# Keys and values of the second layer as two units of seven block products each, with five of the products inside the softmax steps

## The chip, the cores and the metric

The kernel runs on one core of a Trainium2 chip. The metric is the device time of one execution in microseconds (us). The engines are named as the profile names them: PE (TensorE, matrix products), DVE (VectorE), ACT (ScalarE), POOL (GpSimd) and SP (SyncE, which issues most DMA transfers). All arithmetic is in float32. One matmul of the program stands as two records in the trace.

## The reference

Two layers on 256 tokens of width 1024. Each layer is attention, then a layer norm, then a mixture of 32 experts, then a layer norm. The first layer's attention is of another kind; the change lies in the second layer's, which reads in the reference (cut):

```python
def nsa_attention(x, w_in, w_out, pos_k, pos_v, ck_w1, ck_w2, cv_w1, cv_w2, rel_bias):
    proj = x @ w_in
    sizes = [H * d] + [Hkv * d] * 6 + [3 * H]   
    q, kc, vc, ks, vs, kw, vw, g = jnp.split(proj, np.cumsum(sizes)[:-1].tolist(), axis=-1)
    ...
    kcmp = compress(kc, pos_k, ck_w1, ck_w2)
    vcmp = compress(vc, pos_v, cv_w1, cv_w2)
    ...
    return gc[..., 0:1] * o_c + gc[..., 1:2] * o_s + gc[..., 2:3] * o_w
```

There are H = 16 query heads and Hkv = 4 key heads of d = 64. `ks`, `vs` are keys and values of the selected-block branch, `kw`, `vw` those of the sliding-window branch; each is x (256 by 1024) times 256 columns of `w_in`. With 256 tokens each of the two branches sees every earlier token, and they differ in keys and values alone. The compressed branch (15 compressed keys per key head) makes `o_c`.

## The kernel before

**Stages.** Attention of layer 0, experts of layer 0, attention of layer 1, experts of layer 1. SP streams the weights through a ring of six 2 MB slots and some other buffers; a slot is loaded again when its last reader has counted up a semaphore. The fixed loads of layer 1 are numbered 0 to 8: 0 to 2 are the input weights of the units `kv` (compressed keys and values), `qa` and `qb` (queries), 3 and 4 the compression weights, 5 is [ks | vs] (512 columns), 6 is [kw | vw], 7 and 8 the output weights. The slots of 5 and 6 go to gate and up weights of the first expert pair.

**Units.** A product of 512 output columns, 1024 inputs and 256 tokens is cut into 2 by 2 blocks and done with seven block products (`p1`, `p2`, `p6`, `p7`, `p5`, `p3`, `p4`, in that order, `unit_products`, L967) in place of eight. This needs sums of weight blocks on DVE (`t3`, `t1` in place, `t2`, `t4`; `sum_w_blocks`, L1708 to L1717) and sums of x blocks (`s1` to `s4`, made once for the layer). ACT copies `p1` out of its PSUM bank (`copy_product`, L2235), and DVE adds the others up in seven additions (`c11`, `u2`, `u3`, `c22`, `u4`, `c12`, `c21`; `add_products`, L1724). A bank is written again only when the addition that reads it last is done (`result_read`). `kv`, `qa` and `qb` are such units.

**Keys and values.** `ks`, `vs`, `kw`, `vw` are computed in full by `nsa_group(7)` to `nsa_group(10)`, 16 matmuls each: keys with the weights as the stationary operand (`project_T`, L937), values with x as the stationary one (L1533). After group 7 or 9 ACT makes four copies out of PSUM (`nsa_copy`, L2425), since a key head is wanted in both halves of the partitions; after group 8 or 10 DVE makes one (L2145). Groups 7 and 8 run ahead of the softmax steps, between the pieces of the compressed branch: L1586 and L1593 make its keys and values, L1602 its scores, L1612 transposes them for a softmax on DVE and ACT (L2200 to L2211).

**Softmax steps.** `attention(1, ...)` runs 16 steps s, each for two heads and one branch, on all engines as a pipeline. PE: scores of step s (L985, L987) once DVE has read those of s-1 (`scores_read`); then a filler, if the table `beside` has one; then transposes of the probabilities of step s-2 (L1009) and products with the values of s-3 (L1029, L1031). DVE: a pass with bias and maximum over the scores of s (L1678), `scale_job(s-1)` (L1661, L642), what is beside the step, and a copy. ACT: exponentials of s (L2249), what is beside, and a copy. The fillers of PE are group 9 in step 0, the transposes of the compressed probabilities (L1620) and the first half of group 10 in step 1, its second half in step 3, and pieces of the output projection (L1038) from step 7 on. The steps 0 to 3 are (heads 0 and 1, selected), (2 and 3, selected), (0 and 1, window), (2 and 3, window). Every engine runs its program in the order written.

**Sequence of SP.** Expert weights of layer 1 that go to the buffers of bias and scratch wait for the last `scores_read` (L755).

Of the kernel before, what the change touches and what calls it, by code (L numbers as in the profile page):

```python
# [92 lines left out]
def build(nc, x_in, rel_bias, router_w, router_b, ln_g, ln_b, moba_w_in, moba_w_out, nsa_w_in, nsa_w_out,  # L93
# [3 lines left out]
    with ctx:  # L97
# [102 lines left out]
        def unit_operands(w, w_sums, x_sums):  # L200

            (b11, b12), (b21, b22) = w_blocks(w)
# [6 lines left out]
        SHARED_BANKS = {u: {"p1": "p2", "p6": "p7", "p5": "p3"} for u in ("q1", "k1")}  # L209
# [10 lines left out]
        def written(u, p):  # L220
# [5 lines left out]
        cmp_sT = work[:, 6144:7168].rearrange("p (b n) -> p b n", b=2)  # L226
# [3 lines left out]
        NSA_UNITS = {"kv": 1.0, "qa": DH ** -0.5, "qb": DH ** -0.5}  # L230
# [9 lines left out]
        unit_w_sums.update({"kv": [w_rows(softmax_area[:, 1024 * n:1024 * (n + 1)]) for n in (1, 2, 3)],  # L240
                            "qa": [w_rows(work[:, 1024 * n:1024 * (n + 1)]) for n in (2, 3, 4)],
                            "qb": [w_rows(softmax_area[:, 1024 * n:1024 * (n + 1)]) for n in (1, 2, 3)]})
# [177 lines left out]
        loaded = [sem(f"loaded{s}") for s in range(NSLOT + 5)]  # L420
        def count_of(*order):
# [19 lines left out]
            ("qb", ("p1",)))  # L441
# [15 lines left out]
            ("qb", ("t3", "t1", "t2", "t4")))  # L457
        product_done, product_copied, product_added = sem("product_done"), sem("product_copied"), sem("product_added")
        w_summed, x_summed = sem("w_summed"), sem("x_summed")
        for u, n in (("kv", 0), ("qa", 1), ("qb", 2)):  # L460
            unit_w[u] = slot8(ring_use["fixed", 1, n, 0])
        unit_of.update({u: unit_operands(unit_w[u], unit_w_sums[u], nsa_x_sums) for u in ("kv", "qa", "qb")})
        for u, n in MOBA_UNITS.items():
            unit_w[u] = slot8(ring_use["fixed", 0, n, 0])
# [69 lines left out]
        for n, g in ((5, 3), (6, 5)):  # L534
            fixed_freed[1][n] = (proj_ready[1], g)
# [85 lines left out]
        def ends_heads(l, j):  # L621
# [5 lines left out]
        ADDS_BEHIND = {FOUR: ("c11", "u2", "u3"), THREE: ("c22", "u4", "c12", "c21")}  # L627
        beside = [{0: [("proj", ("q1", FOUR))], 1: [("proj", ("q1", THREE))], 2: [("proj", ("k1", FOUR))], 3: [("proj", ("k1", THREE))],
                   5: [("out", 0)], 6: [("out", 1)], 7: [("out", 2)], 8: [("out", 3)], 9: [("out", 4)], 10: [("out", 5)]},
                  {0: [("proj", 9)], 1: [("cmp", 0), ("half", 10)], 3: [("proj", 10)], 7: [("out", 0)], 8: [("out", 1)], 10: [("out", 2)], 12: [("out", 3)],  # L630
# [277 lines left out]
        def _(pe):  # L908
# [39 lines left out]
            def unit_products(u, *names):  # L948

                for p in names:  # L950
# [13 lines left out]
                    at = unit_at(u, p)  # L964
# [1510 lines left out]
```

## Time and profile before

| | |
|---|---|
| median of 3 runs | 1195.28 us (1195.17 to 1195.92) |
| profiled execution | 1194.18 us, span of its instructions 1192.4 us |
| PE busy in the span | 1010.8 us (85%) |
| DVE, ACT, POOL busy | 342.9, 184.7, 55.7 us |
| HBM read | 446.72 MB |
| layer-1 attention up to the softmax steps | about 583 to 651 us |
| softmax steps of layer 1 | about 651 to 722 us |

The profile's page gives totals, the span in 40 slices of 29.8 us, and the costliest groups. The trace gives single instructions in order of time, the chain of work that ended last, and busy times of chosen stretches. Times in the trace count from the span's start. The granted clock is 1.00 for 2.4 GHz and 0.50 for 1.2 GHz.

### The profile page before, as it was taken

How to read it: one execution, taken by the hardware profiler on the slowest of the kernel's cores; microseconds unless marked ns; L12 is line 12 of the kernel's file. 1: busy time of each engine (PE TensorE's matmuls, PEld its weight loads, DVE VectorE, ACT ScalarE, POOL GpSimd, SP SyncE). 2: the span in 40 equal slices, each digit the busy share in tenths (PEclk: the TensorE clock that was granted, in tenths of full speed). 3: DMA queues.
4: the chain of work that ended last, by engine and by line, in shares of the span. 5: the costliest groups of instructions: out<-in, count | busy, mean ns of one | idle time of the engine just before them, and what ended most of it. 6: DMA issues, size and time to landing. Idle time of an engine off the chain costs nothing.

```text
span 1192.4 us, 18810 instructions
## 1 busy us (share of the span) xinstructions
PE 1010.8 (85%) x7832; PEld 565.2 (47%) x7832; DVE 342.9 (29%) x868; ACT 184.7 (15%) x474; POOL 55.7 (5%) x133
## 2 busy tenths in 40 slices
PE   9999999976698966678899999999966888865766
PEld 7595544543343533343698655444533433433432
DVE  4745612221111111111563675313211111111112
ACT  1023211100010100000321662110100010100002
POOL 1012010000000000000100220100000000000000
PEclk9999999997799988789999999999988899978889
DMA  9937999999999999999993609999999999999995
GB/s 355 370 142 291 344 393 419 425 427 427 427 427 429 427 427 428 426 426 422 375 363 135 234 10 371 374 421 426 425 429 428 426 427 428 427 427 429 427 426 225
DMA packets 59350, 449.08 MB, mean 377 GB/s; under 512 B 4580, under 2 KB 10981, under 8 KB 32637
## 3 DMA queue, kind: packets, MB, share of 16 engines
q1 hardware_dynamic: 57248, 442.52, 90.3%
q0 software_dynamic: 1680, 4.88, 1.1%
q8 instruction: 66, 1.08, 0.4%
q10 hardware_dynamic: 332, 0.42, 0.1%
q14 instruction: 24, 0.19, 0.0%
HBM read 446.72 MB, written 1.07 MB: 376 GB/s over the span
## 4 chain that ended last, share of the span: by engine, by line
PE 55%; DMA 41%; DVE 2%; issue 1%; SPq 1%; ACT 1%; DVEq 0%
PE bank L1187 15%; DMA ring<-in_moe_w_down 14%; DMA ring<-in_moe_w_up 11%; DMA ring<-in_moe_w_gate 10%; PE bank L967 6%; PE bank L1151 5%; PE bank L1038 5%; DMA bias<-in_moe_w_up 5%; PE bank L1272 3%; PE bank L1248 2%; PE bank L1436 2%; PE bank L1287 2%; PE bank L1009 1%; PE bank L1533 1%; PE bank L937 1%; PE bank L1259 1%
## 5 line engine op out<-in xcount | busy, mean ns | idle before, releaser
L1187 PE MATMUL bank<-ring,work 128*32 128x256 f32 (+1 forms) x2656 | 331.0, 483 | 108.9 <-DMA ring<-in_moe_w_up 36.2
L1187 PEld LDWEIGHTS bank<-ring,work 128*32 128x32 f32 (+1 forms) x2656 | 152.4, 133 | 242.2 <-issue 211.8
L1899 DVE TENSOR_TENSOR work<-work,bank 128x256 f32<-128x256 f32 (+1 forms) x32 | 15.6, 488 | 520.0 <-PE bank L1187 520.0
L1272 PE MATMUL bank<-ring,work 128*32 128x512 f32 x576 | 91.0, 613 | 11.3 <-DMA ring<-in_moe_w_down 6.9
L1187 PE MATMUL bank<-softmax_area,work 128*32 128x256 f32 (+1 forms) x352 | 66.2, 506 | 34.4 <-DMA ring<-in_moe_w_gate 25.6
L1912 DVE TENSOR_TENSOR xs<-xs,bank 128x512 f32<-128x512 f32 x112 | 71.0, 682 | 41.4 <-PE bank L1290 23.2
L1187 PE MATMUL bank<-bias,work 128*32 128x256 f32 (+1 forms) x384 | 77.9, 492 | 0.0
L1151 PE MATMUL bank<-work,acc 128*128 128x128 f32 (+1 forms) x448 | 75.5, 323 | 0.0
L1151 PEld LDWEIGHTS bank<-work,acc 128*128 128x128 f32 x448 | 66.0, 191 | 16.6 <-issue 11.5
L1187 PEld LDWEIGHTS bank<-softmax_area,work 128*32 128x32 f32 (+1 forms) x352 | 32.2, 141 | 67.0 <-issue 61.2
L2317 ACT COPY work<-bank 128x256 f32<-128x256 f32 (+1 forms) x32 | 13.6, 426 | 321.5 <-PE bank L1224 252.3
L1038 PE MATMUL bank<-ring,work 128*128 128x512 f32 x128 | 59.3, 604 | 0.5 <-DVE work L1671 0.5
L2249 ACT ACTIVATE softmax_area<-softmax_area,neg_max 128x128 f32<-128x128 f32 x96 | 42.5, 443 | 64.4 <-DVE neg_max L1678 64.4
L1290 PE MATMUL bank<-work 64*128 64x512 f32 x192 | 47.7, 615 | 2.8 <-ACT work L2337 2.8
L2312 ACT ACTIVATE work<-bank 128x256 f32<-128x256 f32 (+1 forms) x32 | 14.0, 437 | 219.6 <-PE bank L1187 219.6
L1272 PEld LDWEIGHTS bank<-ring,work 128*32 128x32 f32 x576 | 23.7, 112 | 47.1 <-issue 37.8
L1917 DVE COPY work<-bank 128x256 f32<-128x256 f32 (+1 forms) x28 | 15.1, 539 | 96.3 <-PE bank L1151 96.2
L1038 PEld LDWEIGHTS bank<-ring,work 128*128 128x128 f32 x128 | 22.9, 189 | 26.9 <-issue 25.5
L1224 PEld LDWEIGHTS bank<-tab,work 64*64 64x64 f32 x384 | 25.4, 210 | 21.4 <-issue 17.3
L1678 DVE CUSTOM_DVE_ANT_0 softmax_area<-bank,bias 128x128 f32<-128x128 f32 x96 | 28.6, 353 | 10.8 <-PE bank L987 10.5
L1224 PE MATMUL bank<-tab,work 64*64 64x64 f32 x384 | 28.1, 284 | 3.6 <-DVE work L1899 2.2
L1187 PEld LDWEIGHTS bank<-bias,work 128*32 128x32 f32 (+1 forms) x384 | 31.1, 135 | 0.0
(322 smaller groups left out, 1264.7 us busy)
## 6 DMA issues: line engine op xcount, KB each, us to landing
ring<-in_moe_w_gate SPq DMA_DIRECT2D x44, 2048.0 KB, 29.8
ring<-in_moe_w_up SPq DMA_DIRECT2D x40, 2048.0 KB, 28.9
ring<-in_moe_w_down SPq DMA_DIRECT2D x36, 2048.0 KB, 29.1
softmax_area<-in_moe_w_down SPq DMA_DIRECT2D x8, 2048.0 KB, 25.8
ring<-in_moe_w_down SPq DMA_DIRECT2D x12, 1024.0 KB, 8.1
ring<-in_moe_w_gate SPq DMA_DIRECT2D x12, 1024.0 KB, 8.8
bias<-in_moe_w_gate SPq DMA_DIRECT2D x6, 2048.0 KB, 34.3
softmax_area<-in_moe_w_up SPq DMA_DIRECT2D x6, 2048.0 KB, 28.1
```

The costliest lines, as they stand in the source:

```text
L967: last = mm(bank[b][:, at + n * P:at + (n + 1) * P], w[:, t, n * P:(n + 1) * P], x[:, t, :], start=(t == 0), stop=(t == HALF_K - 1))
L1038: return mm(bank[2 * tt + n][:, :], oT[:, m, tt * P:(tt + 1) * P], out_weights(l, m)[:, n * 512:(n + 1) * 512], start=(m == 0), stop=(m == ...
L1151: last = mm(bank[b][:, n * slots:(n + 1) * slots], xsP[:, tt, t, :], pick[:, tt, 0:slots], start=(tt == 0), stop=(tt == 1))
L1187: last = mm(bank[2 + k][row:row + cap, 0:width], xgT_of(group_of[i])[:, t, at + e * cap:at + (e + 1) * cap], w[e](t)[:, part * width:(part ...
L1224: last = mm(bank[4][at, m * 64:(m + 1) * 64], hid[at, m:FF // 2:FT], ident[at, at], start=True, stop=True)
L1248: last = mm(bank[5 + n][e * CAP_WIDE:(e + 1) * CAP_WIDE, :], hidT[:, m, e * CAP_WIDE:(e + 1) * CAP_WIDE], w[e](m)[:, n * 512:(n + 1) * 512 ...
L1272: last = mm(bank[5][row:row + CAP_NARROW, :], hidT_narrow[:, m, CAP_NARROW * e:CAP_NARROW * (e + 1)], w[e](m)[:, n * 512:(n + 1) * 512], s ...
L1287: mm(bank[b][:, :], picksT(i)[:, tt, :], y_slot[:, n * 512:(n + 1) * 512], start=True, stop=True).then_inc(spread_ready[l], 1)
L1290: mm(bank[b][:, :], pick_wT[rows_n, tt, :], y_slot[rows_n, 0:512], start=i < PAIRS - 1, stop=True).then_inc(spread_ready[l], 1)
L1678: last = v.tensor_tensor_reduce(out=probs[:, 2 * (s % 3) + a, x:y], in0=bank[2 + a][:, x:y], in1=bias_for(2 * m + a, tt), scale=-1.0, scal ...
L1912: v.tensor_tensor(c, c, bank[b][:, :], ALU.add).then_inc(acc_added[l], 1)
L2249: last = s_.activation(pr, pr, ACT.Exp, bias=neg_max[:, s % 3, a, tt:tt + 1], scale=-1.0, accum_out=job_sum[:, s % 3, a, tt:tt + 1])
```

## The change

Keys of both branches become one unit `keys` (256 columns of load 5 beside 256 of load 6), values a unit `values`. Of `keys`, p1, p2 and p6, p7, p4 run ahead of the softmax steps, of `values` p1, p2 and p6, p7; the fillers are p5, p3 of `keys` in step 0, p4 of `values` in step 1 and p5, p3 of `values` in step 3. `values` has x as the stationary operand and 256 moving columns. The additions follow another order (`add_joint_products`), so that the selected branch (c11, c21) is ready first. ACT spreads the key heads over the partitions with three copies from SBUF to SBUF for each branch. The weight sums of both units, eight of 1024 elements, are put among the work of DVE. In step 0 of layer 1, `scale_job(0)` comes behind the additions. The line numbers below are those of the changed kernel, L1001 and L996 standing for L967, L1726 to L1735 for L1708 to L1717, L1742 for L1724.

```diff
-        SHARED_BANKS = {u: {"p1": "p2", "p6": "p7", "p5": "p3"} for u in ("q1", "k1")}
+        SHARED_BANKS = {u: {"p1": "p2", "p6": "p7", "p5": "p3"} for u in ("q1", "k1", "keys", "values")}
...
-        cmp_sT = work[:, 6144:7168].rearrange("p (b n) -> p b n", b=2)
+        cmp_sT = softmax_area[:, 1024:2048].rearrange("p (b n) -> p b n", b=2)
...
+            "keys": {"p1": (0, ("qb", "p3")), "p2": (0, None), "p6": (1, ("qb", "p5")), "p7": (1, None),
+                     "p4": (0, ("keys", "p2")), "p5": (1, ("values", "p2")), "p3": (1, None)},
+            "values": {"p1": (1, ("keys", "p7")), "p2": (1, None), "p6": (0, ("keys", "p4")), "p7": (0, None),
+                       "p4": (0, ("values", "p7")), "p5": (1, ("keys", "p3")), "p3": (1, None)}})
...
+        both = [slot8(ring_use["fixed", 1, n, 0]) for n in (5, 6)]
+        for u, at in (("keys", 0), ("values", 2 * P)):
+            unit_w[u] = [[w[:, HALF_K * k:HALF_K * (k + 1), at:at + 2 * P] for w in both] for k in range(2)]
...
-        for n, g in ((5, 3), (6, 5)):
-            fixed_freed[1][n] = (proj_ready[1], g)
+        fixed_freed[1][5] = (product_done, products_through("values", "p2"))
+        fixed_freed[1][6] = (product_done, products_through("values", "p3"))
...
-                  {0: [("proj", 9)], 1: [("cmp", 0), ("half", 10)], 3: [("proj", 10)], 7: [("out", 0)], 8: [("out", 1)], 10: [("out", 2)], 12: [("out", 3)],
+                  {0: [("proj", ("keys", REST))], 1: [("proj", ("values", LAST_SELECTED)), ("cmp", 0)], 3: [("proj", ("values", REST))], 7: [("out", 0)], 8: [("out", 1)], 10: [("out", 2)], 12: [("out", 3)],
...
             unit_products("qb", "p7", "p5", "p3", "p4")
+            for n in (5, 6):
+                arrived(1, n)
+            unit_products("keys", "p1", "p2")
             pe.wait_ge(chidT_ready, 1)
...
-            nsa_group(7)
+            unit_products("keys", "p6", "p7", "p4")
             pe.wait_ge(ckv_ready, 1 + GROUP)
...
-            nsa_group(8)
+            unit_products("values", "p1", "p2")
             pe.wait_ge(csT_dve, 1)
             pe.wait_ge(csT_act, 1)
...
             last.then_inc(cs_ready, 1)
+            unit_products("values", "p6", "p7")
...
+            def add_joint_products(u, *names):
...
+                    if name == "c11":
+                        dve.wait_ge(product_done, written(u, "p2"))
+                        dve.wait_ge(product_copied, copies_through(u, "p1"))
+                        add(c11, "p2", c12)
+                    elif name == "u2":
+                        dve.wait_ge(product_done, written(u, "p7"))
...
+                        add(c12, "p6", c12)
+                    elif name == "u3":
...
+                        add(c22, "p7", c12)
+                    elif name == "c21":
+                        dve.wait_ge(product_done, products_through(u, "p4"))
...
-            add_products("qb", "c11", "u2", "u3", "c22", "u4", "c12", "c21")
+            add_products("qb", "c11", "u2", "u3")
+            weights_here(5)
+            weights_here(6)
+            dve.wait_ge(chid_psum, 1)
+            sum_w_blocks("values", "t3", "t1", "t2")
+            add_products("qb", "c22", "u4")
+            sum_w_blocks("values", "t4")
+            sum_w_blocks("keys", "t3")
+            sum_w_blocks("keys", "t1")
+            add_products("qb", "c12", "c21")
+            sum_w_blocks("keys", "t2")
+            add_joint_products("keys", "c11")
+            dve.wait_ge(product_done, products_through("qb", "p4"))
+            sum_w_blocks("keys", "t4")
...
+            def spread_keys(b):
+
+                act.wait_ge(product_added, adds_through("keys", ("c21", "c12")[b]))
+                for half in (slice(DH, P), slice(0, DH)):
+                    s_.copy(nsa_kT[half, b, 2:4, :], nsa_kT[DH:P, b, 0:2, :]).then_inc(keys_spread, 1)
+                act.wait_ge(keys_spread, 2 * b + 2)
+                s_.copy(nsa_kT[DH:P, b, 0:2, :], nsa_kT[0:DH, b, 0:2, :]).then_inc(proj_act[1], 1)
```

**DVE behind the addition u3 of `qb`** (bank5), before: the additions c22, u4, c12 and c21 of `qb`, then the copies of the compressed keys and values.

```order
L1724 SCALAR_TENSOR_TENSOR work<-bank5,work 128x2x128 [waits product_added,product_done]
L1724 SCALAR_TENSOR_TENSOR work<-bank1,work 128x2x128 [waits product_added,product_done]
L1724 SCALAR_TENSOR_TENSOR work<-bank1,work 128x2x128
L1724 SCALAR_TENSOR_TENSOR work<-bank0,work 128x2x128 [waits product_added,product_done]
L1724 SCALAR_TENSOR_TENSOR work<-bank5,work 128x2x128 [waits product_added,product_done]
L2186 COPY nsa_area<-bank4 128x80 [waits ckv_psum]
L2189 COPY nsa_area<-bank5 15x256 x4
```

The same place with the change, where L1726, L1729, L1732 and L1735 are weight sums:

```order
L1742 SCALAR_TENSOR_TENSOR work<-bank5,work 128x2x128 [waits product_added,product_done]
L1726 TENSOR_TENSOR acc<-ring 128x1024 [waits chid_psum,loaded5,loaded3]
L1729 TENSOR_TENSOR ring<-ring 128x4x256 [waits w_summed]
L1732 TENSOR_TENSOR softmax_area<-ring 128x1024 [waits w_summed]
L1742 SCALAR_TENSOR_TENSOR work<-bank1,work 128x2x128 [waits product_added,product_done]
L1742 SCALAR_TENSOR_TENSOR work<-bank1,work 128x2x128
L1735 TENSOR_TENSOR acc<-ring,softmax_area 128x1024 [waits w_summed]
L1726 TENSOR_TENSOR softmax_area<-ring 128x1024
L1729 TENSOR_TENSOR ring<-ring 128x4x256 [waits w_summed]
L1742 SCALAR_TENSOR_TENSOR work<-bank0,work 128x2x128 [waits product_added,product_done]
L1742 SCALAR_TENSOR_TENSOR work<-bank5,work 128x2x128 [waits product_added,product_done]
L1732 TENSOR_TENSOR softmax_area<-ring 128x1024 [waits w_summed]
```

Six weight sums now stand between u3 and c12 of `qb` (the row on bank0), and a seventh behind c21 (bank5).

**PE from p4 of `qb` on**, before: L1586 and L1593 are the compressed keys and values, L937 is group 7, L1602 the compressed scores.

```order
L967 MATMUL bank5<-xT,softmax_area 128x128 [waits w_summed,product_added]
L967 MATMUL bank5<-xT,softmax_area 128x128 x7
L1586 MATMUL bank4<-nsa_area 64x128 [waits chidT_ready]
L1586 MATMUL bank4<-nsa_area 64x128 x3
L1593 MATMUL bank5<-nsa_area 15x64 [waits product_added]
L1593 MATMUL bank5<-nsa_area 15x64 x31
L937 MATMUL bank1<-xT,ring 128x256 [waits loaded3,product_added]
L937 MATMUL bank1<-xT,ring 128x256 x15
L1602 MATMUL bank2<-work,nsa_area 32x256 [waits ckv_ready]
L1602 MATMUL bank2<-work,nsa_area 32x256 x7
L1602 MATMUL bank3<-work,nsa_area 32x256 x8
```

With the change (L1001 products, L1602 and L1609 the compressed keys and values):

```order
L1001 MATMUL bank5<-xT,softmax_area 128x128 [waits w_summed,product_added]
L1001 MATMUL bank5<-xT,softmax_area 128x128 x7
L1001 MATMUL bank0<-xT,ring 128x128 [waits product_added,loaded5,loaded3]
L1001 MATMUL bank0<-xT,ring 128x128 x15
L1602 MATMUL bank4<-nsa_area 64x128 [waits chidT_ready]
L1602 MATMUL bank4<-nsa_area 64x128 x3
L1609 MATMUL bank5<-nsa_area 15x64 [waits product_added]
L1609 MATMUL bank5<-nsa_area 15x64 x31
L1001 MATMUL bank1<-work,softmax_area 128x128 [waits x_summed,w_summed,product_added]
L1001 MATMUL bank1<-work,softmax_area 128x128 x7
L1001 MATMUL bank1<-work,softmax_area 128x128 [waits x_summed]
L1001 MATMUL bank1<-work,softmax_area 128x128 x7
```

p1 and p2 of `keys` are put ahead of the compressed keys; p1 goes to bank0, so it waits for the addition c12 of `qb`.

**DVE at the end of the compressed softmax**, before: L2202 subtracts the maximum, ACT takes exponentials, L2204 to L2211 normalise, L1678 opens step 0.

```order
L2202 TENSOR_TENSOR work<-work,cmp_max 128x32x15 [waits dve_chain]
L2204 TENSOR_REDUCE cmp_sum<-work 128x32 [waits cs_exp]
L2205 RECIPROCAL cmp_sum<-cmp_sum 128x32 [waits dve_chain]
L2207 TENSOR_TENSOR cmp_sum<-cmp_sum,nsa_area 128x32 [waits dve_chain]
L2210 TENSOR_TENSOR work<-work,tab 128x16x15 [waits dve_chain] x2
L2211 TENSOR_TENSOR work<-work,cmp_sum 128x32x15 [waits dve_chain]
L1678 ISA softmax_area,neg_max<-bank2,bias 128x128 [waits scores_ready_1,bias_reloaded]
```

With the change:

```order
L2264 TENSOR_TENSOR work<-work,cmp_max 128x32x15 [waits dve_chain]
L1777 SCALAR_TENSOR_TENSOR work<-bank0,work 128x256 [waits product_added,product_done]
L1777 SCALAR_TENSOR_TENSOR work<-bank0,work 128x256 [waits product_added]
L2267 TENSOR_REDUCE cmp_sum<-work 128x32 [waits cs_exp]
L2268 RECIPROCAL cmp_sum<-cmp_sum 128x32 [waits dve_chain]
L2270 TENSOR_TENSOR cmp_sum<-cmp_sum,nsa_area 128x32 [waits dve_chain]
L2273 TENSOR_TENSOR work<-work,tab 128x16x15 [waits dve_chain] x2
L2274 TENSOR_TENSOR work<-work,cmp_sum 128x32x15 [waits dve_chain]
L1694 ISA softmax_area,neg_max<-bank2,bias 128x128 [waits scores_ready_1,bias_reloaded]
```

The additions u2 and u3 of `values` (L1777) stand between the subtraction and the sum, and wait for p7 of `values`.

## Rows read from the trace of the kernel before

**Rows 1.** The page: granted clock and DMA share in 40 slices of the span.

```profile
PEclk9999999997799988789999999999988899978889
DMA  9937999999999999999993609999999999999995
```

**Rows 2.** Stretch: start:end, length, busy time by engine, clock, DMA share, GB/s.

```profile
840.00:900.00 60.00, 44.45 (x468) 24.27 (x466) 8.55 (x18) 5.56 (x12) 0.00 (x0) 0.89 1.01 427
```

**Rows 3.** SP in order of time (start, duration): first expert load behind the softmax steps.

```profile
713.39 0.35 SPq L755 DMA_DIRECT2D bias<-in_moe_w_down  x1
```

**Rows 4.** Chain of work that ended last, in order of time: start, us, what.

```profile
625.18 7.15 PE bank L967 x64
632.33 0.59 PE bank L1586 x8
632.91 1.02 PE bank L1593 x64
633.93 7.10 PE bank L937 x32
641.03 1.86 PE bank L1602 x32
642.89 7.10 PE bank L1533 x32
650.00 0.87 PE bank L1612 x8
...
666.33 0.49 PE bank L985 x4
```

**Rows 5.** DVE in order of time: sums and additions of qb.

```profile
614.83 1.22 DVE L1711 TENSOR_TENSOR ring<-ring 128x1024 f32<-128x1024 f32 x1
...
627.00 0.43 DVE L1724 SCALAR_TENSOR_TENSOR work<-bank,work 128x256 f32<-128x256 f32 x1 [1.58 <-PE bank L967]
628.79 0.76 DVE L1724 SCALAR_TENSOR_TENSOR work<-bank,work 128x256 f32<-128x256 f32 x2 [1.36 <-PE bank L967]
630.58 0.42 DVE L1724 SCALAR_TENSOR_TENSOR work<-bank,work 128x256 f32<-128x256 f32 x1 [1.03 <-PE bank L967]
```

**Rows 6.** Issue of load 6 on SP, and, from the DMA view, its time to landing.

```profile
605.10 8.25 SPq L669 DMA_DIRECT2D ring<-in_nsa_w_in  x1
...
ring<-in_nsa_w_in SPq DMA_DIRECT2D x1, 2048.0 KB, 19.7
```

**Rows 7.** DVE and ACT in order of time, compressed softmax to step 1; ACT copies.

```profile
653.81 0.65 DVE L2204 TENSOR_REDUCE cmp_sum<-work 128x32 f32<-128x480 f32 x1 [0.67 <-ACT work L2445]
656.58 0.28 DVE L1678 CUSTOM_DVE_ANT_0 softmax_area<-bank,bias 128x128 f32<-128x128 f32 x1
659.91 0.67 DVE L642 TENSOR_SCALAR softmax_area<-softmax_area,job_scale,nsa_area 128x128 f32<-128x128 f32 x2
...
657.81 0.40 ACT L2249 ACTIVATE softmax_area<-softmax_area,neg_max 128x128 f32<-128x128 f32 x1 [4.03 <-DVE neg_max L1678]
...
659.57 2.34 ACT L2425 COPY work<-bank 64x512 f32<-64x512 f32 x4
...
732.90 2.06 ACT L2295 COPY acc<-xs 128x1024 f32<-128x1024 f32 x1
```

**Rows 8.** PE behind three pauses (idle time in brackets), and two stretches around such pauses.

```profile
863.33 3.66 PE L1187 MATMUL bank<-ring,work 128*32 128x256 f32 x64 [2.66 <-DMA ring<-in_moe_w_gate]
...
892.71 4.65 PE L1187 MATMUL bank<-ring,work 128*32 128x256 f32 x49 [3.52 <-DMA ring<-in_moe_w_gate]
...
1041.09 0.61 PE L1187 MATMUL bank<-softmax_area,work 128*32 128x256 f32 x1 [4.35 <-DMA ring<-in_moe_w_gate]
...
863.00:869.00 6.00, 3.66 (x64) 2.38 (x64) 0.00 (x0) 0.38 (x1) 0.00 (x0) 1.00 1.01 431
...
889.00:900.00 11.00, 5.54 (x65) 3.29 (x64) 0.00 (x0) 0.97 (x2) 0.00 (x0) 0.84 1.01 426
1041.00:1050.00 9.00, 6.40 (x64) 3.25 (x64) 0.00 (x0) 0.38 (x1) 0.00 (x0) 0.68 0.99 421
```

More of the change, by code:

```diff
@@ L259, in unit_c @@
                 return (qT if u == "q1" else kT)[:, first:first + 2, at]
+            if u == "keys":
+                return nsa_kT[:, n, 0:2, at]
+            if u == "values":
+                return nsa_v[:, n, tt, :].rearrange("p (n q) -> p n q", q=P)
             if u == "kv":
@@ L440, in build @@
             ("qa", ("p1",)),
-            ("qb", ("p1",)))
+            ("qb", ("p1",)),
+            ("keys", ("p1",)),
+            ("values", ("p1",)))
         adds_through = count_of(
@@ L964, in unit_products @@
                     at = unit_at(u, p)
+                    if u == "values":
+                        for t in range(HALF_K):
+                            last = mm(bank[b][:, at:at + 2 * P], x[:, t, :], w[:, t, :], start=(t == 0), stop=(t == HALF_K - 1))
+                        last.then_inc(product_done, 1)
+                        continue
                     for n in range(2):
@@ L1019, in attention @@
                             after(pe, o_copied[l], m)
+                            if m == 0:
+                                pe.wait_ge(product_added, adds_through("values", "c21"))
                             for h in range(2 * m, 2 * m + 4):
@@ L1047, in out_piece @@
                 elif m == 0:
-                    pe.wait_ge(proj_dve[1], 3)
-                    pe.wait_ge(proj_act[1], 2)
+                    pe.wait_ge(product_added, adds_through("values", "c12"))
                 pe.wait_ge(o_copied[l], m + 1)
@@ L1636, in compressed @@
                 return mm(ps, cmp_val[at, hkv, :], cmp_pT[at, hkv, :], start=True, stop=False)
-            attention(1, nsa_job, nsa_group, compressed, transpose_cmp)
+            attention(1, nsa_job, nsa_products, compressed, transpose_cmp)
             out_rest(1)
@@ L1762, in beside_step @@
                             sum_w_blocks("k1", "t4")
-                    elif kind == "proj" and k % 2 == 0:
-                        nsa_copy(k)
+                    elif kind == "proj":
+                        add_joint_products(k[0], *(("c21",) if k[1] == LAST_SELECTED else ("c22", "u4", "c12")))
             def add_piece(l, tt, n):
@@ L2189, in _ @@
                 v.tensor_copy(cmp_val[at, :, :].rearrange("p h d -> p (h d)"), bank[5][at, 0:KV * DH]).then_inc(ckv_ready, 1)
+            add_joint_products("keys", "u2", "u3")
             v.memset(cmp_p, 0.0).then_inc(cs_centred, 1)
+            add_joint_products("keys", "c21")
             dve.wait_ge(csT_psum, 1)
             v.tensor_copy(cmp_sT[:, 0, :], bank[2][:, :]).then_inc(csT_dve, 1)
-            nsa_copy(8)
+            add_joint_products("values", "c11")
             dve.wait_ge(cs_ready, 1)
@@ L2419, in _ @@
                 s_.copy(gate_halves[at:at + 3 * HEADS, :], bank[4][at:at + 3 * HEADS, 0:SEQ]).then_inc(gate_copied, 1)
-            def nsa_copy(g):
-                act.wait_ge(proj_ready[1], g - 5)
-                for dst in (0, DH):
-                    for a in range(2):
-                        last = s_.copy(nsa_kT[dst:dst + DH, (g - 7) // 2, 2 * a:2 * a + 2, :].rearrange("p j q -> p (j q)"),
-                                       bank[1][DH * a:DH * a + DH, :])
-                last.then_inc(proj_act[1], 1)
             values = kv_rows[:, 1, :, :].rearrange("p n q -> p (n q)")
```

101 lines of the change are left out of this document (51 added, 50 removed), and 16 rows, old and new, of tables (NSA_UNITS, adds_through, products_through).

## The prediction

> **What bounds the kernel now.** I read first the 40 slices of the page [rows 1]. DMA is near full (9) nearly everywhere, apart from slices 3 and 4 and 22 to 24. The second hole is the attention of layer 1. Slice 24 ends at 715 us: there the DMA engines have filled every free buffer and wait for the softmax steps. Then I read a stretch of the experts behind it [rows 2]: DMA share 1.01, 427 GB/s, PE busy 44 of 60 us. So the experts run at the speed of DMA, and what counts for them is when their stream starts. SP issues its first load of that stream at 713.39, behind the last pass of DVE over scores [rows 3]. Whatever moves that instant moves the end by as much. Third, the chain of waits between 625 and 667 us [rows 4]: the pieces are PE's, each beginning where the one before ends. The attention of layer 1 is bound by PE, without a pause up to the softmax steps. PE's work there is worth its full price, and so is every pause put into it.
>
> **PE work: less in all, more ahead of the softmax steps.** Four products of the seven-product form take 7.15 us, so one takes 1.79; a full group takes 7.10 [rows 4]. `keys` moves 128 columns per matmul as those do: 7 x 1.79 = 12.5. `values` moves 256 columns as groups 7 and 8 do, whose 32 records take 7.10; a product has 8 records, 1.78, seven are 12.4. Sum 24.9 against 4 x 7.10 = 28.4: 3.5 us less. But ahead of step 0 stand nine products, 9 x 1.785 = 16.1, where groups 7 and 8 took 14.2: 1.9 us more. The rest of the gain is in the fillers, and pays only if PE is what the steps wait for.
>
> One doubt on the 128-column form: rows 4 have 0.112 us per 128-column record and 0.222 per 256-column one, the same per column, so loading weights twice as often costs nothing here. The Trainium skill (TensorE: Matmul & The Clock Gate, Back-to-back issue gap) gives for a sustained stream 81 ns at 128 columns against 131 at 512, which is 2.5 times as dear per column. By that ratio, as an estimate from the page, `keys` would take some 30 us instead of 12.5 and the change would lose over 15 us. The rows contradict it, and I leave it out.
>
> **The pause ahead of `keys` p1.** p1 overwrites bank 0 and waits for c12 of `qb`. Before, DVE does c12 at 630.58, ahead of PE's end of p4 at 632.33 [rows 4, 5]. Now DVE starts after u3, at 627.43, on six sums of 1024 elements: 1.22 us each and about 0.03 between them, 7.5 us [rows 5]. The pair c22, u4 adds 0.76 and c12 itself 0.42. It ends at 627.43 + 8.65 = 636.1. PE stands from 632.33 to 636.1: **3.8 us**. The input is not late: load 6 lands at 605.10 + 19.7 = 624.8 [rows 6], 2.6 us ahead of the first sum. Queued behind the waiting matmul is all of PE.
>
> **To step 0.** After that DVE keeps ahead: keys t2 and c11, t4 and the five copies end near 644, while PE needs them at 646.6, behind p4 of `keys`. ACT's three spreading copies start after c21 near 647.5 and, at 0.59 us each (2.34 for four, [rows 7]), end near 649.4; the copy of scores ends at 650, and PE asks at 652.1. So PE goes through. Before, it took 632.33 to 650.87, 18.54 us, to reach step 0 [rows 4]; now 18.54 + 1.9 from 636.1: step 0 at **656.5** (before 650.87). The transposes of compressed scores end 3.55 us earlier (p6, p7 of `values` stand behind them), at 653.0 against 650.87: +2.1 us.
>
> **DVE then becomes the bound.** DVE's compressed softmax follows 2.1 us later than before. ACT's exponentials would release it at 653.81 + 2.1 = 655.9. But now u2 and u3 of `values` are in between and wait for p7, done at 656.5 (+0.2 to be seen): two dependent additions to 657.6. The rest of that softmax took 653.81 to 656.58, 2.8 us [rows 7], so the pass over the scores of step 0 starts at 660.35 instead of 656.58 and ends at 661.5, which is 1.2 later. PE has done its filler by 656.5 + 0.86 + 3.57 = 660.9 and waits 0.6. Before, the filler of 7.10 us covered DVE (PE to 658.8, DVE to 657.7). The three additions behind the pass (about 1.2) lie beside ACT's exponentials (657.81 to 659.7 before, 1.9 long) and cost nothing; without that cover they would cost their 1.2. From the end of that pass to the end of the next one it is 1.9 (ACT) + 0.8 (scaling) + 1.1 = 3.9 us, so step 2 starts at 665.4. The pass of step 2 waits for its scores (0.9) and takes 1.2: step 3 starts at **667.7**, before at 666.33 [rows 4]. The filler of step 3 is as long as the one it replaces (3.55 against half a group). From there on the instructions are the same, except two more additions of DVE that end before its next scores. Loads to the slots of 5 and 6 go out some 2 us later, which the idle DMA of slice 24 hides. Sum of the schedule: **+1.4 us**, the 3.5 us of PE work included. Its error I take as -0.7 to +0.8: a dozen hand-overs of 0.05 to 0.2 us.
>
> **The clock behind the pause.** A pause of 3.8 us doesn't occur in this part of the trace, so I bound it by pauses elsewhere. With 3.52 us before 892.71 it is 0.84 over 889 to 900 [rows 8]: 11 x 0.16 = 1.8 us of clock lost, all but a little of it while PE works again. With 4.35 us before 1041.09 it is 0.68 over 9 us: 2.9 us lost, the highest I find for such a pause. Of the 25 pauses over 3 us in the trace all are followed by a stretch at the lower level (1.2 GHz), of the eight between 2.1 and 2.7 us four are, the 2.66 before 863.33 not. So I expect the fall to 0.50 in or right behind the pause, at a price of 0 to 2.9 us, and take 1.7 (nearest in length: 3.52). PE is the bound from there to the transposes of compressed scores, and DVE and ACT follow PE there, so the loss goes through in full. Against: those 25 are in the expert stages, where PE is less dense before the pause.
>
> **Forecast and rivals.**
> A, forecast: 1.4 + 1.7 = **+3.1 us**. On the profiled execution 1194.2 + 3.1 = 1197.3; it lies 1.1 us under the median of the runs shown, so against that 1195.3 + 3.1 = 1198.4. With its errors +2.4 to +4.6. Chance 0.57.
> B, no fall of the clock: the same schedule, PE at 1.00 throughout, +1.4 us: 1196.7 (+0.7 to +2.3). For it speaks the density before the pause; it decides if the pause is seen as activity enough. This ends as no measurable change. Chance 0.24. The Trainium skill (TensorE: Matmul & The Clock Gate, Part 1: The HAM clock gate) says that activity is judged by a count that runs freely of the kernel, so that the same pause may be judged in two ways; the halves among the short pauses agree.
> C, slow spreading: a copy out of SBUF on ACT is not in the trace in this form. Lower bound 0.59 us (out of PSUM), upper bound the reordering copy of 1024 elements in 2.06 [rows 7], so 1.03 for 512. At 1.03 the three copies of step 0 end at 666.5, 1.1 us after step 2 wants its keys: +2.5 without the clock's fall, +4.2 with it (1199.5). It decides from 0.65 us per copy. I take 0.6, since the 2.06 goes with a strided read. Chance 0.10.
> D, faster: the waits of PE vanish, because the sums are done earlier or c12 isn't held up, and PE's smaller work is what counts: with no pause (-3.8) and no fall, 1.4 - 3.8 = -2.4, and at best the whole -3.5: 1191.8 to 1192.9. It would need c12 by 632.3, that is three sums fewer ahead of it; the order of DVE shows all six. Chance 0.09.
> That the change doesn't do what it says is excluded by the order: the five products stand in steps 0, 1 and 3.
>
> **Numbers.** What a measurement here can tell from no change is about 0.2%, 2.4 us. Slower by over that: A nearly whole and C, 0.62. Within: B, and the low edge of A, 0.29. Faster: D, 0.09. The range runs from 1196.0 (low edge of B) to 1200.0 (A with the dearest fall, C); it leaves out D and a few in 100 above and below.
>
> **What would show it.** A pause of PE of 3.8 us before the first product of `keys`, ended by an addition of DVE. The granted clock near 0.5 for some us between 636 and 644; if it is 1.00, B. Step 0 some 5.6 us later than 650.87 without a fall, 7.3 with it. DVE waiting for p7 ahead of the sum of exponentials, and PE waiting 0.6 us for DVE at step 1. Spreading copies of 0.6 us; if 1.0, C. Step 3 at 667.7 without a fall, 669.4 with it, and the first expert load 3.1 us after 713.39. The forecast falls if the pause is under 2 us, or if the time behind 716 us doesn't shift along.

## The result and the profile of the changed kernel

| | before | changed |
|---|---|---|
| median of 18 runs each, us | 1195.28 | 1198.01 |
| lowest and highest, us | 1194.16 to 1197.67 | 1196.26 to 1202.47 |
| ratio, with its 95% interval | | 1.0028 [1.0020, 1.0036] |
| profiled execution, us | 1194.18 | 1200.75 |

The change makes the kernel 2.7 us slower: the forecast was 3.1 us, 1198.4 in all. The profiled execution of the changed kernel, however, is 6.6 us over that of before, and its runs scatter more. Both have to be explained. Of the experiments below, one execution of `quarter` (2875 us) and one of `quarter_u` (1313 us) were far slower than all others and stand in none of the medians and ratios.

The page first: busy time by engine, then the 40 slices with the granted clock and the DMA share.

```profile
PE 1013.0 (84%) x7872; PEld 567.5 (47%) x7872; DVE 355.9 (30%) x888; ACT 184.6 (15%) x474; POOL 55.7 (5%) x133
...
PEclk9999999987899987789998999999988899977989
DMA  9937999999999999999992609999999999999995
```

Against [rows 1] the DMA line still has its second hole at slices 22 to 24. The experts behind it still run at the speed of DMA, as in [rows 2] (the same view, stretch 840 to 900):

```profile
840.00:900.00 60.00, 47.40 (x468) 24.70 (x472) 8.97 (x19) 6.49 (x14) 0.00 (x0) 0.90 1.01 427
```

So the attention of layer 1 is where to look. PE in order of time, from p4 of `qb` to step 3 (idle time and its releaser in brackets):

```profile
631.30 1.95 PE L1001 MATMUL bank<-xT,softmax_area 128*128 128x128 f32 x16
636.68 6.45 PE L1001 MATMUL bank<-xT,ring 128*128 128x128 f32 x32 [3.43 <-DVE work L1742]
643.07 0.66 PE L1602 MATMUL bank<-nsa_area 128*64 128x128 f32 x8
...
655.64 1.04 PE L1628 MATMUL bank<-tab,softmax_area 128*128 128x128 f32 x8
...
660.07 0.49 PE L1019 MATMUL bank<-work 64*128 64x128 f32 x4
...
664.99 0.49 PE L1019 MATMUL bank<-work 64*128 64x128 f32 x4 [0.23 <-DVE neg_max L1694]
...
671.13 0.49 PE L1019 MATMUL bank<-work 64*128 64x128 f32 x4 [0.42 <-DVE neg_max L1694]
```

Here is the pause ahead of `keys` p1, 3.43 us, ended by an addition of DVE. Behind it p1 and p2 take 6.4 us, and four products took 7.15 in [rows 4]: these two run at little over half speed. The clock says so too. Stretches of the same trace, with the granted clock third from the end:

```profile
632.00:636.00 4.00, 1.25 (x12) 1.06 (x10) 3.97 (x6) 0.00 (x0) 0.00 (x0) 0.93 0.35 78
636.00:640.00 4.00, 3.32 (x15) 3.35 (x16) 2.00 (x4) 0.00 (x0) 0.00 (x0) 0.50 1.02 417
640.00:644.00 4.00, 4.00 (x52) 3.71 (x53) 0.34 (x1) 0.38 (x1) 0.00 (x0) 0.72 0.10 34
644.00:648.00 4.00, 4.00 (x84) 3.89 (x71) 2.95 (x7) 0.00 (x0) 0.00 (x0) 1.00 0.02 4
```

It is at the lower level (1.2 GHz, 0.50) over 636 to 640 and in part of the stretches beside it. How long in all, a longer stretch tells. First that of this trace, then the same of the trace of `quarter`, an experiment further down, for comparison:

```profile
634.00:644.00 10.00, 7.32 (x65) 7.06 (x68) 4.30 (x6) 0.38 (x1) 0.00 (x0) 0.66 0.58 211
```

```profile
634.00:644.00 10.00, 7.99 (x113) 7.62 (x114) 5.32 (x9) 0.39 (x1) 0.00 (x0) 0.83 0.53 206
```

A mean of 0.66 over 10 us, made of 1.00 and 0.50 alone, is 6.8 us at 0.50 here (from 635.4 to 642.2); 0.83 is 3.4 us in `quarter`. DVE in the pause:

```profile
628.27 1.22 DVE L1726 TENSOR_TENSOR acc<-ring 128x1024 f32<-128x1024 f32 x1
...
634.98 1.23 DVE L1729 TENSOR_TENSOR ring<-ring 128x1024 f32<-128x1024 f32 x1
636.12 0.75 DVE L1742 SCALAR_TENSOR_TENSOR work<-bank,work 128x256 f32<-128x256 f32 x2
```

Between the first sum at 628.27 and the pair c12, c21 at 636.12, DVE works without a hole, and PE waits for it. The first expert load on SP, which answers to [rows 3]:

```profile
718.20 0.35 SPq L784 DMA_DIRECT2D bias<-in_moe_w_down  x1
```

**One measure for all kernels.** What PE does up to the end of p4 of `qb` is the same in all of them, but its end lies at 631.9 to 633.1 us, depending on the execution. (Where a pause follows, I take the end at 1.79 us behind the start of p4's last 16 matmuls, as it is where the next product follows at once; here 631.30 + 1.79 = 633.09.) The two rows of before on which this rests, in the same view of PE:

```profile
632.25 0.66 PE L1586 MATMUL bank<-nsa_area 128*64 128x128 f32 x8
...
650.80 0.49 PE L985 MATMUL bank<-work 64*128 64x128 f32 x4
```

The chain of [rows 4] puts both instants 0.07 to 0.08 us later; I keep to this view. In before the matmul behind p4 is of another form and starts 1.87 us behind the start of p4's last 16, not 1.79, so that differences to before are uncertain by 0.1 us. I therefore measure from there to the first expert load. Before: 713.39 - 632.25 = 81.14 us. Changed: 718.20 - 633.09 = 85.11, 4.0 more. The other 2.6 us of the 6.6 are not part of the change: 0.8 us had been lost ahead of it, and 1.8 us is scatter of the time behind the load, which was 479.0 us in before's trace, 480.8 in this one, and 479.0 to 481.6 over all the traces of this study; its cause is not traced. From step 3 to the load it is 47.06 us before (713.39 - 666.33) and 47.07 changed (718.20 - 671.13), so nothing happens there: the 4.0 us arise between 633 and 671.

### The profile page after: what moved, and what is told of

Same layout as the page of the kernel before. It is cut to its first block, busy times and chain, and to the rows that moved or that the text cites. A ratio compares the mean times of both kernels' runs of the same rounds, so it can differ in the third digit from the quotient of the medians.

```text
span 1199.0 us, 18921 instructions
## 1 busy us (share of the span) xinstructions
PE 1013.0 (84%) x7872; PEld 567.5 (47%) x7872; DVE 355.9 (30%) x888; ACT 184.6 (15%) x474; POOL 55.7 (5%) x133
## 4 chain that ended last, share of the span: by engine, by line
PE 52%; DMA 42%; DVE 3%; issue 1%; ACT 1%; SPq 1%; DVEq 0%
DMA ring<-in_moe_w_down 16%; PE bank L1220 14%; DMA ring<-in_moe_w_up 11%; DMA ring<-in_moe_w_gate 10%; PE bank L1001 7%; DMA bias<-in_moe_w_up 5%; PE bank L1072 5%; PE bank L1184 4%; PE bank L1305 3%; PE bank L1281 2%; PE bank L1469 2%; PE bank L1320 2%; PE bank L1041 1%; PE bank L1292 1%; PE bank L1496 1%; PE bank L1063 1%
## 5 line engine op out<-in xcount | busy, mean ns | idle before, releaser
L1220 PE MATMUL bank<-ring,work 128*32 128x256 f32 (+1 forms) x2656 | 327.2, 477 | 111.9 <-DMA ring<-in_moe_w_up 39.6
L1305 PE MATMUL bank<-ring,work 128*32 128x512 f32 x576 | 96.0, 633 | 12.5 <-DMA ring<-in_moe_w_down 6.7
L1001 PE MATMUL bank<-xT,ring 128*128 128x128 f32 x224 | 29.4, 294 | 3.6 <-DVE work L1742 3.4
```

The lines of the kernel that those rows point to most:

```text
L1001: last = mm(bank[b][:, at + n * P:at + (n + 1) * P], w[:, t, n * P:(n + 1) * P], x[:, t, :], start=(t == 0), stop=(t == HALF_K - 1))
L1220: last = mm(bank[2 + k][row:row + cap, 0:width], xgT_of(group_of[i])[:, t, at + e * cap:at + (e + 1) * cap], w[e](t)[:, part * width:(part ...
L1305: last = mm(bank[5][row:row + CAP_NARROW, :], hidT_narrow[:, m, CAP_NARROW * e:CAP_NARROW * (e + 1)], w[e](m)[:, n * 512:(n + 1) * 512], s ...
```

## The theory and its rivals

Mine has three parts. (1) DVE's six sums ahead of c12 make the pause, and the schedule behind it costs 1.3 us net even at full clock. (2) The pause may bring the clock down, for some 2.7 us. (3) Without both, PE's smaller work is a gain of up to 3.5 us. The rivals: the products themselves cost more than counted, so that the change loses wherever the pause is; or the clock costs nothing or falls anyway; or PE's work in the fillers still bounds the steps.

## Experiments on the clock

**The changed kernel once more** (`after2`), on the same chip as `warm`, `c12first` and `late_u`. (The other four experiments ran on another, with a run of before of their own.)

> The changed kernel again, on the same chip as the others: ratio 1.0028, pause ahead of keys p1 of 3.4 us, and a fall of the clock of 3.4 or 6.8 us behind it.

Measured 1197.40 us (before 1195.13), ratio 1.0024 [1.0014, 1.0034]. This time the profiled execution had no fall. PE, the same places:

```profile
636.23 3.81 PE L1001 MATMUL bank<-xT,ring 128*128 128x128 f32 x32 [3.43 <-DVE work L1742]
639.97 0.66 PE L1602 MATMUL bank<-nsa_area 128*64 128x128 f32 x8
...
656.97 0.49 PE L1019 MATMUL bank<-work 64*128 64x128 f32 x4
...
661.89 0.49 PE L1019 MATMUL bank<-work 64*128 64x128 f32 x4 [0.22 <-DVE neg_max L1694]
...
668.03 0.49 PE L1019 MATMUL bank<-work 64*128 64x128 f32 x4 [0.42 <-DVE neg_max L1694]
```

The pause is the same to the last digit, 3.43 us, and p1 and p2 take 3.74 us (636.23 to 639.97) instead of 6.39. From the end of p4 (632.65) to the first expert load (715.10) it is 82.45 us, 1.3 over before. So one kernel has two faces: 4.0 us lost where the clock falls as in the first profile, 1.3 where it doesn't, and the difference, 2.7 us, is what p1 and p2 lose. The expectation had a fall here too; it doesn't come in every execution. The median of the runs lies between the two.

**Matmuls in the pause** (`warm`): the same kernel, with four matmuls of 512 columns (eight records) on an unused bank between p4 of `qb` and p1 of `keys`.

```diff
             unit_products("qb", "p7", "p5", "p3", "p4")
             for n in (5, 6):
                 arrived(1, n)
+            keep_warm(4)
             unit_products("keys", "p1", "p2")
```

> The changed kernel with four matmuls of 512 columns on a bank nobody needs put into the pause ahead of the first product of keys; nothing else differs. They last 3.4 us and should fit into the pause. Theory (schedule +1.1 to +1.4 us, clock the rest): no fall of the clock behind the pause, keys p1 and p2 back from 6.4 to 3.6 us, time about 1196.5, ratio to the kernel before 1.0010, 1.5 to 2 us under the changed kernel. Rival (the clock costs nothing that reaches the end, the pause and DVE's lateness are all of it): no change against the changed kernel, ratio 1.0025 to 1.0030.

Measured 1196.74 us, ratio 1.0010 [1.0001, 1.0019].

```profile
633.13 3.60 PE L1120 MATMUL bank<-tab 128*128 128x512 f32 x8
636.63 3.84 PE L1001 MATMUL bank<-xT,ring 128*128 128x128 f32 x32
```

The products start no earlier, since DVE's c12 still comes when it comes, but they run at full speed, and the measured stretch is 82.41 us, the same as in `after2`. On the median this is worth 0.7 us against `after2` and 1.3 against the first measurement of the changed kernel. The time against before is as expected (1.0010); the gain of 1.5 to 2 us over the changed kernel was not reached. That it is less than 2.7 fits a fall that comes in only some of the executions. The intervals of `warm` and `after2` overlap, so this pair alone doesn't settle it.

**The pause made longer** (`long`): one weight sum of `keys` done two more times, ahead of c12. **The same with matmuls in it** (`long_warm`): seven of them, 14 records.

```diff
             sum_w_blocks("values", "t4")
+            for _ in range(2):
+                link(v.tensor_tensor(unit_w_sums["keys"][1], unit_w["keys"][1][1], unit_w["keys"][0][1], ALU.subtract))
             sum_w_blocks("keys", "t3")
```

> The changed kernel with two more weight sums of 1024 elements (a block sum made three times over) ahead of c12 of qb, so that PE's pause is 5.9 us instead of 3.4. Theory (a pause costs its length, and the lower clock behind it another 1.4 to 2.9 us that reach the end; at 3.4 us it falls in some executions, at 5.9 us in all): 1.3 + 2.5 + 2.2, about 1201.1, ratio 1.0050. Rival (the length of the pause is all): 1.3 + 2.5, ratio 1.0032.

> The kernel long with seven matmuls of 512 columns (6.0 us) put into the pause. Theory: the clock stays at 1.00, products of keys at 1.8 us each, ratio 1.0032 (1.3 + 2.5 us), 2.2 us under long. Rival (the clock's price doesn't reach the end): the same time as long.

Measured: `long` 1201.78 us (before 1195.67), ratio 1.0047 [1.0033, 1.0062]; `long_warm` 1199.15, ratio 1.0026 [1.0015, 1.0038]. PE of `long`, then two of its stretches:

```profile
637.95 6.76 PE L1001 MATMUL bank<-xT,ring 128*128 128x128 f32 x32 [5.94 <-DVE work L1742]
```

```profile
636.00:640.00 4.00, 2.05 (x9) 2.08 (x10) 3.23 (x5) 0.00 (x0) 0.00 (x0) 0.66 0.77 315
640.00:644.00 4.00, 4.00 (x20) 4.00 (x20) 0.00 (x0) 0.00 (x0) 0.00 (x0) 0.50 0.00 0
```

PE of `long_warm`:

```profile
632.84 6.17 PE L1120 MATMUL bank<-tab 128*128 128x512 f32 x14
638.85 3.84 PE L1001 MATMUL bank<-xT,ring 128*128 128x128 f32 x32
```

Two sums of 1.22 us lengthen the pause by 2.5 us (5.94 against 3.43), and `long_warm` shows a stretch 2.5 us longer than `warm` (84.92 against 82.41): time of DVE ahead of c12 goes to the end at its full price. The clock's fall behind a pause is a price of its own, 2.6 us on the medians of this pair, and p1 and p2 show 6.7 us against 3.8. The two intervals overlap a little ([1.0033, 1.0062] and [1.0015, 1.0038]), with six runs of `long`; it is the medians, 2.6 us apart where 2.2 was expected, and the two traces together that speak for the fall. Part 2 holds. The rival that the clock falls anyway is out: between 600 and 725 us the clock falls in four of the five traces with a pause (not in `after2`; those of `quarter` and `quarter_u`, at the end, count among the five) and in none of the five without one (before, `warm`, `long_warm` and the two that follow).

## Experiments on the order of DVE

**c12 ahead of the sums** (`c12first`): nothing is added or left out; DVE does one weight sum between two additions of `qb`, and the sum t4 of `values` goes behind the copies of the compressed keys. Two sums now stand ahead of c12 instead of six.

```diff
...
-            sum_w_blocks("values", "t3", "t1", "t2")
+            sum_w_blocks("values", "t3")
             add_products("qb", "c22", "u4")
-            sum_w_blocks("values", "t4")
-            sum_w_blocks("keys", "t3")
-            sum_w_blocks("keys", "t1")
-            add_products("qb", "c12", "c21")
-            sum_w_blocks("keys", "t2")
+            sum_w_blocks("values", "t1")
+            add_products("qb", "c12")
+            sum_w_blocks("values", "t2")
+            add_products("qb", "c21")
+            sum_w_blocks("keys", "t3", "t1", "t2")
             add_joint_products("keys", "c11")
...
+            sum_w_blocks("values", "t4")
             add_joint_products("keys", "u2", "u3")
```

> The changed kernel with DVE's weight sums put between and behind the additions of qb, so that c12 of qb is done before PE ends p4 of qb. Theory: the pause and the fall of the clock vanish, step 3 starts 2.4 us ahead of the kernel before, time about 1192.9, ratio 0.9980. Rival (the sums are work of DVE that must be paid somewhere: keys t2, t4 or values t4 come late and PE waits for them instead): ratio 0.9995 to 1.001.

Measured 1193.56 us (before 1195.13), ratio 0.9985 [0.9974, 0.9996]: 1.6 us faster than before on the medians, where 1192.9 was expected. DVE does c12 well ahead of the end of p4 (632.79):

```profile
631.22 0.42 DVE L1743 SCALAR_TENSOR_TENSOR work<-bank,work 128x256 f32<-128x256 f32 x1
```

PE:

```profile
632.79 3.74 PE L1002 MATMUL bank<-xT,ring 128*128 128x128 f32 x32
636.45 0.66 PE L1603 MATMUL bank<-nsa_area 128*64 128x128 f32 x8
...
653.46 0.49 PE L1020 MATMUL bank<-work 64*128 64x128 f32 x4
...
658.37 0.49 PE L1020 MATMUL bank<-work 64*128 64x128 f32 x4 [0.22 <-DVE neg_max L1695]
...
664.53 0.49 PE L1020 MATMUL bank<-work 64*128 64x128 f32 x4 [0.42 <-DVE neg_max L1695]
```

There is no idle time in brackets at p1. From the end of p4 to step 0 it is 20.67 us; before it was 18.55 (632.25 to 650.80), so the two more products cost 2.1 us here and nothing else does. To step 3 it is 31.74 us, before 34.08: 2.3 us gained, and the first load comes 78.81 us behind p4 instead of 81.14. Against `after2` this is 3.6 us, the whole of the pause (3.58 from the end of p4, 632.65, to p1 at 636.23). So the seven-product form is no loss in itself: part 3 holds, and the rival that the products are dearer than counted is out.

**And u2, u3 of `values` out of the compressed softmax** (`late_u`): as `c12first`, and these two additions follow DVE's pass over the scores of step 0.

```diff
...
+                    if s == 0 and l == 1:
+                        add_joint_products("values", "u2", "u3")
                     beside_step(l, s)
...
-            add_joint_products("values", "u2", "u3")
             dve.wait_ge(cs_exp, 1)
```

> As c12first, and u2, u3 of values moved out of the compressed softmax into step 0, behind DVE's pass over the scores. Theory (DVE's wait for p7 of values inside the compressed softmax holds up steps 0 to 2): 1.1 us less than c12first, step 3 starts 3.5 us ahead of the kernel before, about 1191.8, ratio 0.9971. Rival (PE bounds step 0 by itself, so DVE's wait is hidden): the same as c12first.

Measured 1193.01 us, ratio 0.9978 [0.9968, 0.9988]: 2.1 us under before on the medians. It is the lowest median, but its interval overlaps that of `c12first` in most of its width, and the runs can't tell the two apart. In the traces the gain over `c12first` is 0.57 us, half of the 1.1 expected. DVE and then PE:

```profile
655.91 0.28 DVE L1696 CUSTOM_DVE_ANT_0 softmax_area<-bank,bias 128x128 f32<-128x128 f32 x1
```

```profile
653.59 0.49 PE L1021 MATMUL bank<-work 64*128 64x128 f32 x4
...
654.44 3.84 PE L1003 MATMUL bank<-work,ring 128*128 128x128 f32 x32
658.21 0.49 PE L1021 MATMUL bank<-work 64*128 64x128 f32 x4
...
664.09 0.49 PE L1021 MATMUL bank<-work 64*128 64x128 f32 x4 [0.50 <-DVE neg_max L1696]
```

DVE's pass now starts 2.3 us behind the scores of step 0 (653.59); in the changed kernel it was 3.7 (660.07 to 663.74). But the filler of 3.84 us and the scores keep PE busy up to 658.21, and PE no longer waits at step 1. In `c12first` it waited 0.22 us there and 0.20 at step 2, and these two are most of the 0.57 us. The time that DVE gained beyond that lay beside PE's work and was worth nothing.

## Experiments on PE's part in the fillers

**A quarter of the filler's matmuls** (`quarter`): p5 and p3 of `keys` in step 0 take one instead of four blocks of the contraction, so the keys are incomplete, and with them the choice of experts later on; I read it up to the first expert load. Its whole time can hold a difference behind that load too, and is weaker evidence.

```diff
+                    used = 1 if u == "keys" and p in ("p5", "p3") else HALF_K
                     for n in range(2):
-                        for t in range(HALF_K):
+                        for t in range(used):
...
-                                      start=(t == 0), stop=(t == HALF_K - 1))
+                                      start=(t == 0), stop=(t == used - 1))
```

> The changed kernel without three quarters of the matmuls of p5 and p3 of keys, the filler of step 0 (the keys of the window branch and half of those of the selected one are not complete). PE has 2.7 us less to do there. Theory (DVE's late compressed softmax sets when step 1 starts, PE waits for it): 0.2 us less than the changed kernel at most, ratio 1.0023 to 1.0028. Rival (PE is the bound of step 0): 2.7 us less, ratio 1.0003.

**The same with u2, u3 of `values` moved** (`quarter_u`), as in `late_u`.

> As quarter, and u2, u3 of values moved out of the compressed softmax to behind DVE's pass over the scores of step 0. Theory: DVE's pass comes 1.2 us earlier and, with PE out of the way, steps 1 to 3 as well: 1.1 us under quarter, ratio 1.0016. Rival (the wait for p7 is hidden): the same as quarter.

Measured: `quarter` 1199.12 us, ratio 1.0031 [1.0020, 1.0042]; `quarter_u` 1197.31, ratio 1.0005 [0.9994, 1.0015]. With 2.7 us less work, PE gained nothing in `quarter`: it waited longer for DVE. PE:

```profile
636.01 5.44 PE L1002 MATMUL bank<-xT,ring 128*128 128x128 f32 x32 [3.42 <-DVE work L1743]
641.38 0.66 PE L1603 MATMUL bank<-nsa_area 128*64 128x128 f32 x8
...
659.24 1.16 PE L1002 MATMUL bank<-work,ring 128*128 128x128 f32 x8
663.29 0.73 PE L1020 MATMUL bank<-work 64*128 64x128 f32 x4 [2.90 <-DVE neg_max L1695]
...
664.81 2.96 PE L996 MATMUL bank<-acc,xT 128*128 128x256 f32 x8
```

The wait at step 1 grows from 0.22 to 2.90 us: in the changed kernel the filler of step 0 is cover beside DVE's chain and PE's work there is worth nothing. What I had not expected are the first line and the last. The stretch from 663 us on:

```profile
663.00:667.00 4.00, 3.71 (x14) 2.67 (x15) 3.12 (x15) 3.64 (x11) 1.20 (x2) 0.57 0.91 367
```

Behind the wait of 2.90 us the clock was down again. The eight matmuls of p4 of `values`, 1.99 us in the other traces, take 2.96, and the scores of step 1 0.73 instead of 0.49. The first line shows that the first fall was a shorter one than in the changed kernel: p1 and p2 take 5.37 us (636.01 to 641.38), 1.6 over the 3.74 of `after2`, not 2.7. With that the sum comes out. Step 1 starts 30.86 us behind p4 and in `after2` 29.24, later by just this 1.6 us; from there to the load it is 54.58 us against 53.21, 1.4 us for the second fall. Together the stretch from p4 to the load is 4.3 us over before; without the two falls it would be what `after2` has. In `quarter_u` DVE's pass starts earlier, the wait is 1.56 us, and no second fall follows:

```profile
661.82 0.49 PE L1021 MATMUL bank<-work 64*128 64x128 f32 x4 [1.56 <-DVE neg_max L1696]
```

Its stretch is 1.6 us over before with a first fall in it that costs 1.6 as well, 2.8 us under `quarter`; about half of that is the clock's, half DVE's. I had expected the gain of DVE's earlier pass alone, and the ratio of 1.0016 was missed.

## All in one table

From the end of p4 of `qb` to the first expert load, in the profiled execution of each kernel; the clock is that seen over the 4 us behind the pause, with the time spent at the lower level.

| kernel | pause, us | clock behind it | stretch, us | against before | ratio of the runs |
|---|---|---|---|---|---|
| before | none | 1.00 | 81.14 | | 1 |
| changed, first profile | 3.43 | 0.50 (6.8 us) | 85.11 | +4.0 | 1.0028 |
| changed, second profile | 3.43 | 1.00 | 82.45 | +1.3 | 1.0024 |
| `warm` | filled | 1.00 | 82.41 | +1.3 | 1.0010 |
| `long` | 5.94 | 0.50 (6.8 us) | 87.9 | +6.8 | 1.0047 |
| `long_warm` | filled | 1.00 | 84.92 | +3.8 | 1.0026 |
| `c12first` | none | 1.00 | 78.81 | -2.3 | 0.9985 |
| `late_u` | none | 1.00 | 78.24 | -2.9 | 0.9978 |
| `quarter` | 3.42 | 0.57 (3.4 us), and again at 663 (3.4 us) | 85.4 | +4.3 | 1.0031 |
| `quarter_u` | 3.42 | 0.60 (3.4 us) | 82.7 | +1.6 | 1.0005 |

## Why the prediction was right, step by step

The total was right, and most of its steps too. Two terms of the schedule were mis-sized by 0.2 to 0.3 us and offset each other; the clock's term was right only as a mean of unlike cases. I put each time against the end of p4, 632.33 in the prediction's rows and 632.65 in the trace of `after2`.

- **The pause**: predicted 3.8 us, counted from the instant at which the next product could start; by the same count it was 3.59 (633.09 to 636.68; the 3.43 in brackets counts from the modelled end of p4). The durations of the additions and sums overlap by about 0.1 us at each change from one kind to the other: from 628.27 to the end of c12 near 636.54 it is 8.3 us instead of the summed 8.65.
- **PE's work**: predicted 1.79 us for a product, measured 1.83 (two in 3.66 in `c12first`). The two more ahead of step 0 cost 2.1 us, 1.9 predicted. The doubt on the 128-column form is answered too: p1 and p2 in 3.66 us are 0.114 us per record, so it is no dearer per column. (Its sum, redone, comes to a loss of some 15 us, where the prediction has over 15.) The gain that can be had is 2.9 us in `late_u`, of 3.5; the longer products explain 0.3 of the rest, hand-overs may hold the remainder, which I haven't traced.
- **Step 0**: 24.2 us behind p4 predicted, 24.32 measured. The pause was 0.2 shorter and the work on the way, 20.74 us instead of 20.44, 0.3 longer.
- **DVE becomes the bound**: right. The wait for p7 is there, and it is put down to PE in the trace of the changed kernel; the second row is the pass over scores that follows.

```profile
660.17 0.88 DVE L1777 SCALAR_TENSOR_TENSOR work<-bank,work 128x256 f32<-128x256 f32 x2 [1.23 <-PE bank L996]
...
663.74 0.28 DVE L1694 CUSTOM_DVE_ANT_0 softmax_area<-bank,bias 128x128 f32<-128x128 f32 x1
```

  The pass of step 0 starts 27.99 us behind p4 in `after2`, 28.02 predicted. PE waits 0.22 us at step 1 instead of 0.6, since its filler shows 3.84 us and not 3.57.
- **Step 3**: 35.37 predicted, 35.38 measured; the schedule's sum +1.4 predicted, +1.3 measured.
- **The clock**: that a fall would follow was right for most executions, its price was not the one I took. I took 1.7 us from the pause of 3.52 us in [rows 8], with 2.9 as the dearest. In the first profile the price was 2.7. The difference is how long the clock stays down while PE works: 11 x 0.16 = 1.8 us lost in the stretch 889 to 900 is 3.5 us at 0.50, and in the changed kernel it was 6.8 us. A fall of 3.4 us is what `quarter` and `quarter_u` had behind the same pause, and there it cost 1.6, near the 1.7; the 2.9 of the stretch 1041 to 1050 goes with 5.8 us at 0.50. And it doesn't fall every time: with a pause of 3.42 or 3.43 us it did in three of four profiled executions. So the same pause cost 0, 1.6, 1.6 and 2.7 us, and my 1.7 came out well because it lies among them; that the medians agree is in part luck. The better form would have been several cases of one kernel, each with its share, instead of A and B as cases of which one is true. The Trainium skill (TensorE: Matmul & The Clock Gate, Part 1: The HAM clock gate) says that activity is judged by a count that runs freely of the kernel. By that rule the same pause can be judged in two ways; the traces of the changed kernel and `after2`, 3.43 us both and 0.50 against 1.00, agree.
- **C, slow spreading copies**: out. ACT of the changed kernel:

```profile
650.82 1.25 ACT L2304 COPY work<-work 64x512 f32<-64x512 f32 x2 [7.26 <-DVE work L1777]
652.10 0.62 ACT L2306 COPY work<-work 64x512 f32<-64x512 f32 x1
```

  0.62 us each, where 0.60 was taken and 0.65 was the point of decision.
- **D, faster**: not in this order of DVE. Its condition, c12 by the end of p4, and its price of -2.4 are what `c12first` shows: -2.3 in the trace, -1.6 on the medians.
- **The load behind the steps**: 3.1 us later was predicted; it was 4.0 with the fall of the first profile and 1.3 without. The time from step 3 to it was unchanged, 47.07 us, as was the rule that the end moves with it, within the scatter of some 2 us behind the load.

Left open: why the time behind the first load varies by 2.6 us between executions, in what share of its executions the changed kernel's clock falls, and why it stays down for 3.4 us in one and 6.8 in another.

## What to carry to other kernels

A form with fewer products trades TensorE's time for sums on another engine, and the place of these sums decides its sign: here the same instructions cost 2.7 us or gain 1.6 (medians), by whether four of them stand ahead of an addition that frees a bank. List what the product behind the join waits for, and put the sums between those additions, not ahead of them. Where a pause of about 3 us in a dense stretch can't be avoided, matmuls on a free bank kept the clock up here (`warm`, `long_warm`), but they repair only the clock's part of the loss; and before cutting the work of an engine, see whether it is what the step waits for, since a cut that only makes the engine idle can cost time.

## What the runs showed of the hardware

- The same pause of 3.43 us in the same program left the clock at 1.00 in one execution and brought it to 0.50 in another; a pause of 2.90 us between two steps did so once, waits of 1.56 us and less in the attention of layer 1 did not in these traces.
- The price of a fall was about half of the time that PE worked at the lower level: 2.7 us behind a pause of 3.43 us and 2.9 behind one of 5.94 (6.7 us against 3.8 for the same two products), where the clock was down for 6.8 us, and 1.6 twice behind one of 3.42 us, where it was down for 3.4. The length of the pause did not decide it alone.
- Less work on PE brought nothing and a second fall: with 2.7 us less in the filler of step 0, the trace of `quarter` has step 1 where it would be anyway and loses 1.4 us behind it. The runs (1.0031, and 1.0028 and 1.0024 with all the work) don't tell the kernels apart, so this rests on one trace.
